# Modulation blocks at other places, weight splits three tiles ahead, and a reordered output projection in a two-block transformer

## The reference

```python
def first_block(x, ...):
    h = rms_norm(x, attn_norm_w)
    r_q, r_k, r_v, r_g, c_q, c_kv, k_pe = split(h @ w_in)
    mixed = concat([retention_group(...), mla_group(...)])
    x = x + mixed @ w_out                                # output projection
    h = rms_norm(x, ffn_norm_w)
    u = causal_conv3(h @ w_up) + conv_b                  # up projection, 2 x 2816 columns
    x = x + (silu(u[..., :2816]) * u[..., 2816:]) @ w_down   # down projection
    return rms_norm(x, final_norm_w)

def second_block(x, c, ctx, c_ctx, ada_w, ada_b, ...):
    for i in range(2):
        # modulation: six vectors of 1024 from a 1024 x 6144 matrix
        sh1, sc1, g1, sh2, sc2, g2 = split(silu(c) @ ada_w[i] + ada_b[i], 6)
        hx = x * (1 + sc1) + sh1
        y = mixer_ab(hx, hc, ...) if i == 0 else mixer_pool(hx, ...)
        x = layer_norm(alpha * x + g1 * y)
        f = peer(x * (1 + sc2) + sh2, peer_wq[i], peer_keys[i], peer_u[i], peer_v[i])
        x = layer_norm(alpha * x + g2 * f)               # peer: 16384 experts
    return x
```

## Time and profile before

| | before |
|---|---|
| median of 3 runs (lowest to highest) | 2334.12 us (2333.29 to 2335.51) |
| the profiled execution | 2331.67 us |
| its span in the trace | 2330.4 us |
| mean granted clock of PE | 0.992 |
| busy: PE, DVE, ACT, POOL | 2258.4, 1867.9, 1196.8, 167.1 us |
| chain of waits that ended last, by engine | PE 83%, DVE 10%, ACT 3%, DMA 2%, issue 2% |

### The profile page before, as it was taken

How to read it: one execution, slowest core, us unless ns; L and a number is a source line. 1 busy time by engine, 2 the same in 40 slices (tenths; PEclk the granted TensorE clock), 3 DMA queues, 4 the chain that set the end, 5 groups by cost and what they waited for, 6 DMA issues and landing times.

```text
span 2330.4 us, 34757 instructions
## 1 busy us (share of the span) xinstructions
PE 2258.4 (97%) x13446; PEld 1887.7 (81%) x13446; DVE 1867.9 (80%) x3365; ACT 1196.8 (51%) x1754; POOL 167.1 (7%) x75
## 2 busy tenths in 40 slices
PE   8999999998999999999999999999999999999997
PEld 7889977776788888887777877788888888777786
DVE  7679996568688988888887888769988888887656
ACT  7555554356456565554444445455665554444443
POOL 0000000000034410000000000014430000000000
PEclk9999999999999999999999999999999999999999
DMA  7365593232545555555558896455555555556563
GB/s 277 132 214 201 189 346 117 82 115 89 196 166 185 189 173 172 172 172 172 172 172 307 316 347 214 151 182 190 183 187 169 172 169 173 170 172 239 203 214 130
DMA packets 123508, 442.32 MB, mean 190 GB/s; under 512 B 13760, under 2 KB 16832, under 8 KB 122704
## 3 DMA queue, kind: packets, MB, share of 16 engines
q1 hardware_dynamic: 117464, 425.04, 53.0%
q10 hardware_dynamic: 5880, 15.06, 1.9%
HBM read 436.88 MB, written 3.16 MB: 189 GB/s over the span
## 4 chain that ended last, share of the span: by engine, by line
PE 83%; DVE 10%; ACT 3%; DMA 2%; issue 2%; SPq 0%; ACTq 0%; DVEq 0%
PE psum L433 20%; PE psum L441 14%; PE psum L442 13%; PE psum L443 13%; PE psum L434 10%; PE psum L436 3%; PE psum L2821 3%; DVE low L2558 2%; PE psum L435 1%; DVE cv L2069 1%; DVE acc L1739 1%; ACT cv L1390 1%; ACT spl L1087 1%; PE psum L481 1%; PE psum L2762 1%
## 5 line engine op out<-in xcount | busy, mean ns | idle before, releaser
L2558 DVE TENSOR_TENSOR low<-ring,spl 128x1024 fp32r<-128x1024 f32 x638 | 780.5, 1232 | 277.1 <-ACT spl L1087 275.4
L1087 ACT ACTIVATE spl<-ring 128x1024 fp32r<-128x1024 f32 x702 | 734.6, 1053 | 252.0 <-DMA ring<-in_peer_u 164.3
L433 PE MATMUL psum<-hT,spl 128*128 128x512 f32 x2016 | 730.5, 401 | 1.9 <-DVE hT L1719 1.9
L434 PE MATMUL psum<-hT,low 128*128 128x256 f32 x2016 | 566.7, 281 | 0.0
L433 PEld LDWEIGHTS psum<-hT,spl 128*128 128x128 f32 x2016 | 380.7, 189 | 80.7 <-issue 2.6
L441 PE MATMUL psum<-spl,Ws 128*128 128x512 f32 x1024 | 412.1, 402 | 9.8 <-DVE Ws L2596 9.8
L442 PE MATMUL psum<-low,Ws 128*128 128x512 f32 x1024 | 404.9, 395 | 0.0
L443 PE MATMUL psum<-spl,Ws 128*128 128x512 f32 x1024 | 404.5, 395 | 0.0
L434 PEld LDWEIGHTS psum<-hT,low 128*128 128x128 f32 x2016 | 382.7, 190 | 9.6
L1669 ACT ACTIVATE Ws<-S 128x256 fp32r<-128x256 f32 x256 | 107.1, 419 | 391.8 <-PE psum L443 387.2
L2878 POOL TENSOR_TENSOR low<-ring,spl 128x1024 fp32r<-128x1024 f32 x64 | 160.7, 2513 | 1165.5 <-ACT spl L1087 1165.5
(11 more groups left out here) (413 smaller groups left out, 3046.5 us busy)
## 6 DMA issues: line engine op xcount, KB each, us to landing
ring<-in_peer_u SPq DMA_DIRECT2D x256, 512.0 KB, 3.4
ring<-in_peer_v SPq DMA_DIRECT2D x256, 512.0 KB, 3.5
vring<-in_ada_w SPq DMA_DIRECT2D x56, 512.0 KB, 5.2
ring<-in_w_up SPq DMA_DIRECT2D x44, 512.0 KB, 4.2
aring<-in_ada_w SPq DMA_DIRECT2D x40, 512.0 KB, 5.1
ring<-in_ab_in SPq DMA_DIRECT2D x32, 512.0 KB, 3.5
ring<-in_peer_wq SPq DMA_DIRECT2D x32, 512.0 KB, 4.3
ring<-in_w_down SPq DMA_DIRECT2D x22, 512.0 KB, 4.1
```

The costliest lines, as they stand in the source:

```text
L433: q.matmul(b[:, :].rearrange("p (z t) -> p z t", z=2), l[0], r, start=start, stop=False)
L434: return q.matmul(b[:, 0:256], l[1], r[:, 0], start=False, stop=False)
L1087: q.activation(P.spl[:, m % SLOTS, 0:w], P.ring[:, m % SLOTS, 0:w], ACT.Copy).then_inc(*P.hi.mark(m))
L2558: q.tensor_tensor(P.low[:, n % SLOTS, 0:w], P.ring[:, n % SLOTS, 0:w], P.spl[:, n % SLOTS, 0:w].bitcast(F32), ALU.subtract).then_inc(*P.lo ...
```

## The change

1. The parts go three tiles ahead of PE in place of two, from tile 5 on to the attention's input tiles; those of the attention's projection and of the expert layers stay. In the input projection the two rotations of the retention queries at the end of the second chunk then stand in a row, ahead of the lows of tiles 11 to 13.
2. Steps move: one more in the input projection, one fewer in the output projection, two more (f = 20 and 21) in the up projection, none at the last two tiles of the down projection. In the first value pass they begin at tile 68 in place of 66. The folds go along.
3. A block's load is issued after tile slot+5 in place of slot+6 in the first four stages. In the value passes it stays at slot+5, but the first burst moves from after tile 69 to after tile 67, and the reload of x from before tile 67 to before tile 100.
4. In the output projection DVE and ACT do their parts in another order: the low of the first up tile stands behind the first half's sums.

```diff
-    places = [("in", n) for n in (5, 7, 13, 14, 19, 20)] + [("wo", 4), ("wo", 5)]
-    places += [("up", 2 * f) for f in (2, 4, 6, 9, 11, 14, 16, 18)]
-    places += [("dn", k) for k in range(22)] + [("dn", 8), ("dn", 16)]
+    places = [("in", n) for n in (5, 7, 13, 14, 19, 20, 21)] + [("wo", 4)]
+    places += [("up", 2 * f) for f in (2, 4, 6, 9, 11, 14, 16, 18, 20, 21)]
+    places += [("dn", k) for k in range(20)] + [("dn", 8), ("dn", 16)]
...
-    folds = [("wo_end",), ("up", 42), ("dn", 9), ("dn", 17), ("dn_end",)]
+    folds = [("wo_end",), ("up", 38), ("dn", 9), ("dn", 15), ("dn_end",)]
...
+def ahead(n):
+    return n + (2 if n < 5 else 3)
...
             elif (i, p) == (1, 3):
                 for tb in range(2):
-                    dve_lo(q, P, T_UKV + tb)
                     dve_ret_rope(q, P, 0, tb)
-                dve_lo(q, P, T_UKV + 2)
+                dve_lo(q, P, T_UKV + 3)
...
-    for n in range(6):
-        dve_lo(q, P, T_WO + n + 2)
...
-        dve_ada(q, P, ("wo", n))
-    dve_lo(q, P, T_UP)
...
+    dve_ada(q, P, ("wo", 4))
+    dve_lo(q, P, T_WO + 7)
     q.wait_ge(*P.line("x_loaded").at("x"))
     sums(0, 0)
     sums(0, 1)
+    dve_lo(q, P, T_UP)
...
         if n < 23:
-            dve_lo(q, P, T_UP + 2 * n + 2)
+            dve_lo(q, P, min(T_UP + 2 * n + 3, T_DN + 2))
...
         if n < 22:
-            dve_lo(q, P, T_UP + 2 * n + 3)
+            dve_lo(q, P, T_UP + 2 * n + 4)
             for part in range(2):
                 dve_ada(q, P, ("up", 2 * n + part))
+                dve_ada_cols(q, P, ("up", 2 * n + part - 3))
...
     for k in range(22):
-        dve_lo(q, P, min(T_DN + k + 2, T_DN + 21))
+        dve_lo(q, P, min(T_DN + k + 3, T_DN + 21))
...
-ADA_AFTER = {"in": lambda n: T_IN + n + 6, "wo": lambda n: T_WO + n + 6, "up": lambda n: T_UP + n + 6,
-             "dn": lambda n: T_DN + n + 6}
+ADA_AFTER = {"in": lambda n: T_IN + n + 5, "wo": lambda n: T_WO + n + 5, "up": lambda n: T_UP + n + 5,
+             "dn": lambda n: T_DN + n + 5}
...
-        after[T_PEER[l] + 144 + 69] = [("bias", s0 // 8)] + [("bias", 6)] * (l == 0) + [
+        after[T_PEER[l] + 144 + 67] = [("bias", s0 // 8)] + [("bias", 6)] * (l == 0) + [
...
-            elif n == T_PEER[l] + 211:
+            elif n == T_PEER[l] + 244:
```

More of the change, by code:

```diff
@@ L130, in put @@
         plan.setdefault(slot, []).append((kind, i))
-    places = [("in", n) for n in (5, 7, 13, 14, 19, 20)] + [("wo", 4), ("wo", 5)]
-    places += [("up", 2 * f) for f in (2, 4, 6, 9, 11, 14, 16, 18)]
-    places += [("dn", k) for k in range(22)] + [("dn", 8), ("dn", 16)]
+    places = [("in", n) for n in (5, 7, 13, 14, 19, 20, 21)] + [("wo", 4)]
+    places += [("up", 2 * f) for f in (2, 4, 6, 9, 11, 14, 16, 18, 20, 21)]
+    places += [("dn", k) for k in range(20)] + [("dn", 8), ("dn", 16)]
     places.sort(key=lambda s: (("in", "wo", "up", "dn").index(s[0]), s[1]))
-    places += [("v", 0, 66 + s + s // 5) for s in range(48)] + [("v", 1, 66 + 2 * s) for s in range(8)]
+    places += [("v", 0, 68 + s + s // 5) for s in range(48)] + [("v", 1, 68 + 2 * s) for s in range(8)]
     for s, slot in enumerate(places):
         put("step", s, *slot)
-    folds = [("wo_end",), ("up", 42), ("dn", 9), ("dn", 17), ("dn_end",)]
-    folds += [("v", 0, places[8 * i + 7][2] + 3) for i in range(5, 9)] + [("v_end",), ("v_end",), ("v", 1, 84)]
+    folds = [("wo_end",), ("up", 38), ("dn", 9), ("dn", 15), ("dn_end",)]
+    folds += [("v", 0, places[8 * i + 7][2] + 3) for i in range(5, 9)] + [("v_end",), ("v_end",), ("v", 1, 86)]
     for i, slot in enumerate(folds):
@@ L578, in pe_up_latents @@
         sl = pe_take(q, P, T_UQ + k)
-        q.wait_ge(*dve.at(("cT", 2 * k)))
+        q.wait_ge(*dve.at(("cT", 2)))
         for i, (lo, hi) in enumerate(((0, 480), (480, 768))):
@@ L1149, in act_in @@
             n = in_tile(i, p)
-            act_hi(q, P, n + 2)
-            if n == 1:
+            act_hi(q, P, ahead(n))
+            if n == 2:
                 act_ready_sqrt(q, P, 7)
-            elif n == 2:
                 act_rows(q, P)
@@ L1249, in act_up_latents @@
                 *act.mark(("mq", i, tb)))
-    act_hi(q, P, T_UKV + 2)
+    act_hi(q, P, T_UKV + 3)
     q.wait_ge(*dve.at("rs3"))
@@ L1321, in act_wo @@
     turned(3)
-    act_hi(q, P, T_WO + 2)
+    act_hi(q, P, T_WO + 3)
     square(0)
@@ L1325, in act_wo @@
     square(1)
-    for n in range(6):
[L1327 to L1333, removed]
+    act_hi(q, P, T_WO + 4)
+    q.wait_ge(*rdve.at(("gnb", 1)))
+    q.activation(P.vr, P.vr, ACT.Sqrt).then_inc(*ract.mark("gnsd"))
+    act_hi(q, P, T_WO + 6)
+    turned(0)
+    turned(1)
     act_hi(q, P, T_UP)
@@ L1379, in act_up @@
         if n < 23:
-            act_hi(q, P, T_UP + 2 * n + 2)
+            act_hi(q, P, min(T_UP + 2 * n + 3, T_DN + 2))
         if f >= 1:
@@ L1394, in act_up @@
         if n < 22:
-            act_hi(q, P, T_UP + 2 * n + 3)
+            act_hi(q, P, T_UP + 2 * n + 4)
         if 0 <= f < 22:
@@ L1405, in act_down @@
     for k in range(20):
-        act_hi(q, P, T_DN + k + 2 + (k == 19))
+        act_hi(q, P, T_DN + k + 3)
         act_gates(q, P, ("dn", k))
@@ L1450, in act_ab @@
         for p in range(4):
-            act_hi(q, P, T_AB + 4 * i + p + 2)
+            act_hi(q, P, T_AB + 4 * i + p + 3)
             name, hf = AB_TURN.get((i, p), ("KTc", 0))
@@ L1742, in dve_ada @@
                     *P.ada_dve.mark(("acc", z, i), ("acc", 1, i), ("step", i)))
-    if slot[0] != "v":
+    if slot[0] not in ("v", "up", "dn"):
         dve_ada_cols(q, P, slot)
@@ L1818, in dve_in @@
     dve_lo(q, P, 2)
-    dve_angles(q, P)
     for i in range(5):
@@ L1822, in dve_in @@
             n = in_tile(i, p)
-            dve_lo(q, P, n + 2)
+            dve_lo(q, P, ahead(n))
+            if n == 1:
+                dve_angles(q, P)
             if i == 3 and p < 2:
@@ L2023, in dve_wo @@
     dve_ret_mean(q, P, 0)
-    for n in range(6):
-        dve_lo(q, P, T_WO + n + 2)
[L2026 to L2034, removed]
-        dve_ada(q, P, ("wo", n))
-    dve_lo(q, P, T_UP)
+    dve_lo(q, P, T_WO + 3)
+    dve_ret_mean(q, P, 1)
+    dve_ret_var(q, P, 0)
+    dve_ret_var(q, P, 1)
+    dve_lo(q, P, T_WO + 4)
+    dve_ret_out(q, P)
+    dve_lo(q, P, T_WO + 6)
+    dve_mixed_lo(q, P, 0)
+    dve_mixed_lo(q, P, 1)
+    dve_ada(q, P, ("wo", 4))
+    dve_lo(q, P, T_WO + 7)
     q.wait_ge(*P.line("x_loaded").at("x"))
@@ L2090, in dve_down @@
     for k in range(22):
-        dve_lo(q, P, min(T_DN + k + 2, T_DN + 21))
+        dve_lo(q, P, min(T_DN + k + 3, T_DN + 21))
         dve_ada(q, P, ("dn", k))
+        dve_ada_cols(q, P, ("dn", k - 3))
         if 5 <= k < 21 and k % 2:
@@ L2156, in dve_ab @@
                 evz(i - 1)
-            dve_lo(q, P, T_AB + 4 * i + p + 2)
+            dve_lo(q, P, T_AB + 4 * i + p + 3)
             if (i, p) == (0, 1):
```

## The result

The changed kernel takes 2360.88 us in the median of four runs (2354.73 to 2364.83), the kernel before 2334.82 in four runs beside it: 1.1% slower, ratio 1.011 with a 95% interval of 1.0081 to 1.0138. The forecast was 2348.5, slower; the measured time lies just inside the upper end of the range (2361).

What follows compares the result with a forecast made beforehand. PE is busy nearly throughout, but DVE sets the pace in the up projection. Terms 2 + 1 - 3 + 18 + 4.5 + 4 - 3 - 0.5 - 5.4 - 3.2 = +14.4 us on 2334.12 gave 2348.5 us, range 2330 to 2361.

Steps and rivals of the forecast that it cites:

- The step that decides: Up projection: a held weight load makes DVE wait 2.2 to 2.3 us per step, stretching intervals from 13.00 to 15.2.
- The stage: Up projection as a whole: +18 us, from 15.4 for seven intervals, 2 at the start and 0.6 for the rest.
- 0.6 for the rest: Up projection: 0.6 us added to the sum beside the seven intervals and the start, not itemised.
- The down projection: Down projection: +4.5 us for its late fourth tile, +4 for the loop inside, -3 at its end.
- the rival that I set apart at 0.12: New PE stops also lower the clock: 13 us more, 2362, if all do and nothing absorbs it; chance 0.12.
- The output projection: Output projection: sums start some 2.3 us earlier, the 2.86 us gap falls to about 0.6; -3 us with clock.
- The stretch with the rotations: Input stage: both rotations now stand ahead of the low of tile 11 on busy DVE; +2 us.
- the step at tile 21: Input projection: one more pair of steps where DVE next masks retention scores that PE waits for; +1 us.
- The first expert layer: First value pass: 11 us more for the first block's landing and the reload out of the way; -5.4 us.
- the loop over three tiles: Down projection: step to load to split to low takes 8.8 to 9.2 us against PE's 8.4; +4 with doubled steps.
- the rival "by half": Landing of 3.3 to 4.1 us: up projection costs 4 to 10, sum -8 to +3, 2326 to 2337; chance 0.14.
- The gain at the end of the down projection: Down projection's end: without steps at the last two tiles the 4.12 us gap would go; -3 us kept.

Runs made afterwards that it cites:

- e1: The changed kernel with up-projection block loads back at slot+6 in place of slot+5: 2339.51 us, ratio 1.0018.
- e3: The changed kernel with up-projection weight splits two tiles ahead, as before, and the early block loads kept: 2338.1 us, ratio 1.0010.
- e2: The changed kernel with block loads back at slot+6 in the up and the down projection: 2333.32 us, ratio 1.0002.
- e10: The kernel before with only the reload of x moved from tile 67 to tile 100 of the value passes: 2336.21 us, ratio 1.0005.
- e12: The changed kernel with the first burst of modulation blocks after weight tile 6 in place of 5: 2358.63 us, ratio 1.0098.
- e6: The kernel before with only the steps at the down projection's last two tiles moved to f = 20 and 21 of the up projection: 2336.08 us, ratio 1.0003.

## Why the prediction was right in sign and short in size

*The step that decides was right, in place and in size of the wait.* I had 2.2 to 2.3 us a step and 15.2 us between steps; the trace has 2.08 and 15.17 between the second and the third step, and waits of 2.10 to 2.19 behind the later ones, with the weight load out 0.4 us behind the step and landing in 4.7. e1 and e3 show that it is this loop that stretched the intervals. The Trainium skill ("DMA: Bandwidth & Descriptors", "Anatomy of one DMA — SWDGE (gpsimd) path") would have put the landing at an estimated 4.0 for a block issued right behind another; it gives its fit for transfers that GpSimd issues, and these are issued by SP. Both traces have 4.6 to 5.0, and the measurement decides.

*The stage was undersized, 18 against 22.7.* The first interval was 17.3 us (176.75 to 194.05), not 15.2: there the weight load landed in 6.5 us and DVE waited 4.21. The bias row's load stands between the block's and the weight's there, but in the kernel before it does so too and the weight load landed in 4.7, so the cause of the 6.5 stays open. And "0.6 for the rest" hid a stop that I had not priced: the fold at tile 38 waits for the step of f = 18, which DVE does only after the low two tiles ahead (3.07 us).

*The down projection was undersized, 5.5 against 11.6.* The first stop is 5.54 (I had 4.5), those of the loop 2.04, 1.34, 1.01 and 0.28, 4.7 in all (I had 4), and the end gave 2.3 (I had 3). That makes 7.9. The rest is PE's busy time, which grew by 3.7 us in this stretch (68.96 against 65.26). The clock explains 2.6 of it: it is at the lower level from 332.0 to 338.7, and PE works in the last 5.1 us of that, at half speed. The other 1.1 stays open.

*The clock was the rival that I set apart at 0.12, and it came on top, in part.* I reckoned that a fall would be absorbed, since PE only arrives later at its next stop. In the middle of the up projection that held: from 220 to 240 us the mean clock is 0.93, and the interval from 229.74 to 244.92 is 15.2 us all the same. At the fold, at the start of the down projection and behind the retention masks it did not; that PE has no stop ahead of it to spend there is my reading of it, which no run tests. PE's busy time grew by 12.5 us, near the 13 of that rival. The Trainium skill ("TensorE: Matmul & The Clock Gate", "Part 1: The HAM clock gate") has the clock fall with idling; the trace agrees at 333.58, behind a stop of 5.54 us. Behind the masks the clock fell after a stop of 0.77, and e2, with the same stop and a clock of 1.00, shows that a stop's length alone doesn't tell it.

*That the range holds the time is partly luck.* The forecast's own mechanism had 2339 to 2358, and the median lies above that. The range reached to 2361 only because it took in a part of the clock's rival; two of the four runs lie above it.

*The small terms.* The output projection gave 2.4 and 1.5 of clock (I had 3 in all). The stretch with the rotations cost 2.7 (2), the step at tile 21 0.77 and 3 of clock (1). The first expert layer gave 6.2 (5.4), the second 2.7 (3.2). My reason for the former was mostly wrong: moving the reload alone took 1.2 of the 7.36 us off DVE's wait for the first block (e10). The stop of 4.98 at the start is not the change's: its part of 5 us in the profile is the race of e12.

*Slips in the working.* In the kernel before, DVE came to the held tile 9.4 us after the step (its low begins at 267.20), not 8.2, and DVE does rest there, 0.26 us in each iteration. The terms of the loop over three tiles add up to 8.7 to 9.1 us, not 8.8 to 9.2; with the two doubled steps that makes some 4 to 6, and I took the lower end. The upper end of the rival "by half" comes to +2, not +3. None of these changes the sum.

*The gain at the end of the down projection was right by itself* (the stop went from 4.12 to 1.81, and in e6 to none before the first turn) and wrong as a gain: what was moved opened a task whose accumulator was not free.

## What to carry to other kernels

Where a queue issues in order, a load that waits for an engine holds all that stands behind it; before moving it, count how many of that engine's own steps lie between the step that frees it and the first use of what it holds, and compare with landing time plus splits. A lookahead made longer shortens exactly that distance, so two edits that are free apart, or nearly so, can close a loop together, as they did here. A step that opens a new accumulation carries a wait for the old one: price the wait with the step when it moves.

## What the hardware showed that I had not expected

A stop of 0.77 us was followed by the lower clock level for some 7 us in one profile and by none in another of the same order of work, and over many runs of one kernel the time goes with the mean clock, though not strictly: 9 us between 0.988 and 0.994. A 1 MB load issued 0.03 us behind the start of a 2 MB burst took 11.3 us, and 7.8 us when it was issued 0.6 us ahead of it.
